# A depthwise convolution's products moved from GpSimd to ScalarE, and attention's values transposed one projection tile earlier

## The chip, the cores and the metric

One core of one Trainium2 chip runs the whole program in one launch. The metric is the time of an execution on the device in microseconds (us); of several runs the median is given. The profile is that of one execution.

## What is computed

Two transformer blocks in fp32 on 256 tokens of width 1024. The first block (two kinds of attention, cross-attention to a memory, 16 experts) is not touched. The second has two layers, and each layer's mixer projects its normed input to 2560 columns, from which four parallel mixers are fed. Layer 0 works on 512 tokens (256 of the sequence and 256 of the context), layer 1 on the 256 of the sequence. The change concerns the convolution mixer and, beside it, the projection that feeds all four:

```python
def conformer_conv(u, w_dw, b_dw, ln_g, ln_b):
    a, gate = jnp.split(u, 2, axis=-1)
    h = a * jax.nn.sigmoid(gate)
    h = lax.conv_general_dilated(h, w_dw, window_strides=(1,),
                                 padding=((CONV_K // 2, CONV_K // 2),),
                                 dimension_numbers=('NWC', 'WIO', 'NWC'),
                                 feature_group_count=CONV_CH) + b_dw
    return jax.nn.silu(layernorm(h, ln_g, ln_b))
```

It is depthwise: 256 channels, 31 taps. With the channels in two halves of 128 partitions, each half is a sum of 31 shifted copies of its input, each times one weight per partition.

## The kernel before

Every engine has an instruction list of its own, written out by hand in Python (`@block.tensor`, `@block.scalar`, `@block.vector`, `@block.gpsimd`, and SyncE, which only issues loads); the lists are in order and meet through semaphores. A `Signal` is a semaphore with named counts: `mark` adds to it when an instruction ends, `at` is what a wait needs.

**Projections.** Weights come in tiles of 1024 x 256 fp32, 1 MB each. SyncE loads them in a fixed order into five slots of `raw`, each as soon as the tile five places before is used (`load_tiles`, L617). ScalarE copies a tile to a rounded high part `w_hi` (`act_feed`, L654), VectorE subtracts it for the low part `w_lo` (`dve_feed`, L666), both up to two tiles ahead of TensorE, and TensorE multiplies in three products per chunk (`products`, L677 to L679). The results of a tile stand in one of two pairs of PSUM banks and ScalarE evicts them (`act_tile`, L1640); TensorE may start a tile when the one two places before is evicted. Each layer of the second block has ten such tiles `("win2", l, j)` in the order `W2_ORDER` = 2, 3, 0, 1, 4, 5, 6, 7, 8, 9. Tiles 2 and 3 are the two halves of the convolution's input: after them ScalarE takes the sigmoid (`act_glu`, L2053) and VectorE multiplies (`dve_glu`, L2061) into `conv_in` (`sq` in the profile).

**Convolution.** From place 3 of that order on, VectorE has the taps of the first half of the channels, four or five for every tile, as one multiply-and-add each (`dve_taps`, L1410). GpSimd has those of the second half (`pool_taps`): one multiply with the bias for tap 0 (L1432), then 30 times a multiply into the buffer `term` (L1434) and an add to the sum (L1435), each waiting for the one before. GpSimd does nothing else then. All taps are 512 columns wide in layer 0 and 256 in layer 1; sums and term buffer are parts of `proj`. The layer norm that follows them stands at step 22 of layer 0's attention and step 6 of layer 1's (`plan_layernorm`).

**Values.** Tile 1 holds keys and values of one of the mixers. After the tenth tile TensorE transposes the values (`pe_values_turned`, L2041, four transposes into bank 5), ScalarE copies them out (`act_values`, L2046), and TensorE waits for that copy, for the last tile's eviction, the last rotary embedding and GpSimd's bias (L2420 to L2424) before attention begins.

**Attention.** A unit is a pair of score matrices. At step i (`pe_attention`, `act_attention`, `dve_attention`) TensorE computes the scores of unit i (L1164), transposes the probabilities of unit i-2 (L1181) and multiplies those of unit i-3 with the values (L1198). VectorE takes the maximum of unit i out of PSUM (L1239) and scales the probabilities of unit i-1, for the differential heads with L1260 (one head's map, times minus lambda) and L1262 (the other's, plus the first). ScalarE does the exponentials of unit i (L1211) and copies unit i-2's transposes out (L1223). Between them, at the steps 0 to 7 of layer 0, TensorE multiplies a 1 MB tile of the modulation's weights per step (`pe_ada`, L785), straight from its slot of `raw`; after the eighth the sums go over ScalarE (L811) and back to TensorE (L800). Layer 0 has such tiles again at steps 17 to 20, layer 1 at steps 0 to 3. The first units of layer 0 are those of the context's 256 tokens: eight differential pairs, then eight others.

## Time and profile before

| | us |
|---|---|
| median of three runs | 1669.44 (1666.41 to 1669.54) |
| the profiled execution | 1663.33 |
| its span | 1661.6 |
| TensorE busy | 1593.2 (96%), weight loads 1360.8 (82%) |
| VectorE, ScalarE, GpSimd busy | 891.7, 675.0, 214.9 |
| GpSimd's taps, both layers | 162.5 of these (L1432, L1434, L1435) |
| mean granted clock | 0.988 |

Times in the rows are counted from the start of the span. Engines are PE (TensorE), PEld (its weight loads), DVE (VectorE), ACT (ScalarE), POOL (GpSimd), SP (SyncE). A row such as "L1260 DVE TENSOR_SCALAR work<-work,small 128x256 ... x8 | 9.9, 1242 | 0.3" reads: line, engine, operation, out<-in, shape, count; busy us in total, mean ns of one; the engine's idle time just before them, and after an arrow what ended it. A timeline row has start, duration (from the first start to the last end where it stands for several), and in brackets the idle time before it.

### The profile page before, as it was taken

The page shows a single profiled execution, that of the slowest core. Times are in us where ns is not written, and L with a number is a line of the kernel's source. Part 1 is how long each engine was busy: PE and PEld are TensorE (multiplying, and loading weights), DVE is VectorE, ACT ScalarE, POOL GpSimd, SP SyncE. Part 2 cuts the span into 40 slices and gives each one's busy share as a digit, 9 for nine tenths or more (in the row PEclk, how much of TensorE's full clock was granted, in tenths as well). Part 3 has the DMA queues.
Part 4 walks back from the last instruction along what each step waited for, and adds up shares of the span by engine and source line. Part 5 has one row for each costly group of instructions (what it writes and reads, how often), then busy time and mean ns, then how long its engine had stood idle before and what let it go on. Part 6 is the DMA issues. An engine that isn't in the chain of part 4 may idle for free.

```text
span 1661.6 us, 24572 instructions
## 1 busy us (share of the span) xinstructions
PE 1593.2 (96%) x10537; PEld 1360.8 (82%) x10537; DVE 891.7 (54%) x1198; ACT 675.0 (41%) x974; POOL 214.9 (13%) x206
## 2 busy tenths in 40 slices
PE   7999999999999999978999999999998998899998
PEld 6976997998888888944677888888877975799998
DVE  4623663756544566977725333333327668465554
ACT  5536533444544434146633322221225226543433
POOL 3001000000000016980200000000001860000000
PEclk9999999999999999999999999999999999999999
DMA  9577557566565634373142433233244351355552
GB/s 290 153 250 232 171 176 237 154 188 197 162 206 180 197 88 151 102 228 102 11 117 77 127 102 96 86 98 101 89 139 128 102 170 34 102 178 179 184 181 67
DMA packets 228916, 242.18 MB, mean 146 GB/s; under 512 B 13064, under 2 KB 222440, under 8 KB 228808
## 3 DMA queue, kind: packets, MB, share of 16 engines
q1 hardware_dynamic: 226672, 238.03, 44.7%
q0 software_dynamic: 1600, 2.37, 2.4%
q8 instruction: 83, 1.36, 0.4%
q10 hardware_dynamic: 536, 0.22, 0.1%
q14 instruction: 25, 0.20, 0.0%
HBM read 239.55 MB, written 1.05 MB: 145 GB/s over the span
## 4 chain that ended last, share of the span: by engine, by line
PE 85%; DVE 8%; ACT 4%; issue 1%; DMA 1%; SPq 1%; DVEq 0%; ACTq 0%
PE bank L677 18%; PE bank L679 18%; PE bank L678 18%; PE bank L1817 4%; PE bank L1824 4%; PE bank L1823 3%; PE score_banks L1164 2%; PE score_banks L1890 2%; PE score_banks L1891 2%; PE score_banks L1892 2%; DVE small L1239 2%; PE bank L1198 2%; PE bank L750 1%; PE bank L752 1%; PE bank L751 1%
## 5 line engine op out<-in xcount | busy, mean ns | idle before, releaser
L666 DVE TENSOR_TENSOR w_lo<-raw,w_hi 128x2048 fp32r<-128x2048 f32 (+1 forms) x147 | 338.8, 2307 | 232.6 <-ACT w_hi L654 232.1
L677 PE MATMUL bank<-xn_hi,w_hi 128*128 128x256 f32 (+1 forms) x1232 | 407.3, 331 | 5.5 <-ACT proj L1640 3.1
L678 PE MATMUL bank<-xn_lo,w_hi 128*128 128x256 f32 (+1 forms) x1232 | 404.3, 328 | 0.0
L679 PE MATMUL bank<-xn_hi,w_lo 128*128 128x256 f32 (+1 forms) x1232 | 404.3, 328 | 0.0
L654 ACT ACTIVATE w_hi<-raw 128x2048 fp32r<-128x2048 f32 (+1 forms) x147 | 277.2, 1887 | 156.1 <-PE bank L679 97.8
L677 PEld LDWEIGHTS bank<-xn_hi,w_hi 128*128 128x128 f32 x1232 | 235.7, 191 | 27.5 <-issue 5.0
L678 PEld LDWEIGHTS bank<-xn_lo,w_hi 128*128 128x128 f32 x1232 | 235.9, 191 | 19.9
L679 PEld LDWEIGHTS bank<-xn_hi,w_lo 128*128 128x128 f32 x1232 | 235.7, 191 | 20.0
L677 PE MATMUL bank<-hid_hi,w_hi 128*128 128x256 f32 (+1 forms) x416 | 137.5, 330 | 2.6 <-DVE hid_lo L1722 1.9
L678 PE MATMUL bank<-hid_lo,w_hi 128*128 128x256 f32 (+1 forms) x416 | 136.4, 328 | 0.0
L679 PE MATMUL bank<-hid_hi,w_lo 128*128 128x256 f32 (+1 forms) x416 | 136.4, 328 | 0.0
L1211 ACT ACTIVATE work<-score_banks,small 128x512 f32<-128x512 f32 (+2 forms) x120 | 68.7, 577 | 104.6 <-DVE small L1239 84.2
L1657 DVE SCALAR_TENSOR_TENSOR xT<-bank,mod,xT 128x256 f32<-128x256 f32 x96 | 40.6, 478 | 129.0 <-PE bank L679 116.7
L1640 ACT ACTIVATE proj<-bank 128x512 f32<-128x512 f32 (+1 forms) x60 | 31.4, 558 | 179.2 <-PE bank L679 163.1
L1817 PE MATMUL bank<-w_hi,hid_hi 128*128 128x512 f32 x256 | 102.0, 398 | 0.0
L1239 DVE TENSOR_REDUCE small<-score_banks 128x2 f32<-128x1024 f32 (+3 forms) x64 | 57.9, 905 | 79.9 <-PE score_banks L1164 41.5
L1824 PE MATMUL bank<-w_hi,hid_lo 128*128 128x512 f32 x256 | 100.2, 391 | 0.0
L1793 DVE TENSOR_TENSOR w_lo<-raw,w_hi 128x2048 fp32r<-128x2048 f32 (+1 forms) x36 | 67.0, 1876 | 42.9 <-ACT w_hi L1786 42.8
L677 PEld LDWEIGHTS bank<-hid_hi,w_hi 128*128 128x128 f32 x416 | 79.1, 190 | 11.8 <-DVE hid_lo L1722 3.0
L1434 POOL TENSOR_SCALAR proj<-sq,vec 128x512 f32<-128x512 f32 (+1 forms) x60 | 87.0, 1450 | 5.9
L679 PEld LDWEIGHTS bank<-hid_hi,w_lo 128*128 128x128 f32 x416 | 79.1, 190 | 7.0
L678 PEld LDWEIGHTS bank<-hid_lo,w_hi 128*128 128x128 f32 x416 | 79.1, 190 | 6.7
(336 smaller groups left out, 2724.6 us busy)
## 6 DMA issues: line engine op xcount, KB each, us to landing
raw<-in_w_ada SPq DMA_DIRECT2D x48, 1024.0 KB, 5.7
raw<-in_w_in SPq DMA_DIRECT2D x30, 1024.0 KB, 6.3
raw<-in_w_gate SPq DMA_DIRECT2D x22, 1024.0 KB, 5.4
raw<-in_w_up SPq DMA_DIRECT2D x22, 1024.0 KB, 5.5
raw<-in_w_exp_up SPq DMA_DIRECT2D x16, 1024.0 KB, 7.6
raw<-in_w_exp_gate SPq DMA_DIRECT2D x16, 1024.0 KB, 9.6
raw<-in_w_exp_down SPq DMA_DIRECT2D x16, 1024.0 KB, 5.0
raw<-in_w_down SPq DMA_DIRECT2D x16, 1024.0 KB, 5.2
```

The costliest lines, as they stand in the source:

```text
L654: act.activation(w_hi[:, i % HIGH_SLOTS, 0:k * cols], raw[:, r % RAW_SLOTS, 0:k * cols], ACT.Copy)\
L666: dve.tensor_tensor(w_lo[:, r % RAW_SLOTS, 0:k * cols], raw[:, r % RAW_SLOTS, 0:k * cols], w_hi[:, i % HIGH_SLOTS, 0:k * cols].bitcast(F32 ...
L677: pe.matmul(o, s_hi, m_hi, start=i == 0, stop=False)
L678: pe.matmul(o, s_hi, m_lo, start=False, stop=False)
L679: last = pe.matmul(o, s_lo, m_hi, start=False, stop=i == n - 1)
L1211: last = act.activation(prob(s)[:, 0:nk], score_bank(unit, s)[:, 0:nk], ACT.Exp, bias=nmax(s), accum_out=rsum(s))
L1239: ins = dve.tensor_reduce(nmax(s0, n), src, AX.X, ALU.max, negate=True)
L1434: own.ready(pool.tensor_scalar(term, src(1, k), w, None, ALU.mult))
L1793: last = dve.tensor_tensor(lo, w, hi.bitcast(F32), ALU.subtract)
L1817: pe.matmul(halves_of, x_hi[:, c, ts], hi, start=c == 0, stop=False, skip_group_check=True)
L1823: pe.matmul(halves_of, x_hi[:, c, ts], lo, start=False, stop=False, skip_group_check=True)
L1824: last = pe.matmul(halves_of, x_lo[:, c, ts], hi, start=False, stop=c == KC - 1, skip_group_check=True)
```

## The change

On ScalarE, `act_terms` multiplies the 30 taps 1 to 30 of the second half, in thirteen bunches: before and after the eviction of each of the tiles from place 3 on, but the last, which has only the bunch before. The terms alternate between two buffers in `conv_d` (a part of `proj`); term k waits for the add of term k-2. GpSimd keeps tap 0 and adds each term when it is ready. On TensorE and ScalarE the values are turned and copied after the tile at place 8, the ninth, and TensorE waits for the last tile's eviction at step 1 of attention, behind the scores of the second unit and ahead of that step's modulation products. VectorE's list is the same.

```diff
+VALUES_AT = 8
...
+        def term(l, k):
+            return conv_d[:, k % 2, 0:2 if l == 0 else 1, :]
+
+        def act_terms(act, l, bunch):
+
+            _, _, src = conv_views(l)
+            n = 2 * (len(W2_ORDER) - CONV_FROM) - 1
+            first, last = (1 + (CONV_K - 1) * min(bunch + i, n) // n for i in range(2))
+            if first == 1:
+                act.wait_ge(*dve_misc.at(("glu", l)))
+            for k in range(first, last):
+                w = vec[:, 1, l * 62 + 2 * k + 1:l * 62 + 2 * k + 2]
+                if k >= 3:
+                    act.wait_ge(*term_added.at((l, k - 2)))
+                act.activation(term(l, k), src(1, k), ACT.Copy, scale=w).then_inc(*term_ready.mark((l, k)))
+
         def pool_taps(pool, l):
 
             own = Step(pool, pool_step)
-            ns, acc, src = conv_views(l)
-            term = conv_d[:, 1, 0:ns, :]
-            for k in range(CONV_K):
-                w = vec[:, 1, l * 62 + 2 * k + 1:l * 62 + 2 * k + 2]
-                if k == 0:
-                    b = VEC_AT["conv_b_2"] + 2 * l + 1
-                    own.ready(pool.tensor_scalar(acc(1), src(1, 0), w, vec[:, 0, b:b + 1], ALU.mult, ALU.add))
-                else:
-                    own.ready(pool.tensor_scalar(term, src(1, k), w, None, ALU.mult))
-                    ins = pool.tensor_tensor(acc(1), acc(1), term, ALU.add)
-                    if k < CONV_K - 1:
-                        own.ready(ins)
-            ins.then_inc(*pool_done.mark(("conv", l)))
+            _, acc, src = conv_views(l)
+            w, b = vec[:, 1, l * 62 + 1:l * 62 + 2], VEC_AT["conv_b_2"] + 2 * l + 1
+            own.ready(pool.tensor_scalar(acc(1), src(1, 0), w, vec[:, 0, b:b + 1], ALU.mult, ALU.add))
+            for k in range(1, CONV_K):
+                pool.wait_ge(*term_ready.at((l, k)))
+                pool.tensor_tensor(acc(1), acc(1), term(l, k), ALU.add).then_inc(*term_added.mark((l, k)))
+                pool.wait_ge(*term_added.at((l, k)))
...
-                pe.wait_ge(*pool_done.at(("conv", l)))
+                pe.wait_ge(*term_added.at((l, CONV_K - 1)))
...
-                pe_values_turned(pe, l)
-                pe.wait_ge(*act_out.at(("win2", l, 9)))
+                    if place == VALUES_AT:
+                        pe_values_turned(pe, l)
                 pe.wait_ge(*dve_misc.at(("rope", l, 6)))
                 pe.wait_ge(*act_misc.at(("values", l)))
                 pe.wait_ge(*pool_done.at(("bias", l)))
 
                 def fill(i, l=l):
                     run_plan(l, "pe")(pe, i)
+                    if i == 1:
+                        pe.wait_ge(*act_out.at(("win2", l, W2_ORDER[-1])))
...
-                for j in W2_ORDER:
-                    act_tiles(act, [("win2", l, j)])
+                for place, j in enumerate(W2_ORDER):
+                    act_feed(act, ("win2", l, j))
+                    if place >= CONV_FROM:
+                        act_terms(act, l, 2 * (place - CONV_FROM))
+                    act_tile(act, ("win2", l, j))
                     if j == 3:
                         act_glu(act, l)
-                act_values(act, l)
+                    if place == VALUES_AT:
+                        act_values(act, l)
+                    if place >= CONV_FROM:
+                        act_terms(act, l, 2 * (place - CONV_FROM) + 1)
```

How this moves instructions, at three places. (Lines of the kernel after it are numbered anew: L1640 is L1653 there, L654 is L657, L2046 is L2059, L1435 is L1450, L2041 is L2054, L1164 is L1167, L785 is L788, and L677 to L679 are L680 to L682.)

ScalarE, the last projection tiles of layer 0, before: high parts of weights (L654), evictions (L1640, two pieces a tile, so that x6 is three tiles), values (L2046), then attention's exponentials.

```order
L654 ACTIVATE w_hi<-raw 128x2048
L1640 ACTIVATE proj<-bank 128x512 x2
L654 ACTIVATE w_hi<-raw 128x2048
L1640 ACTIVATE proj<-bank 128x512 x2
L654 ACTIVATE w_hi<-raw 128x2048
L1640 ACTIVATE proj<-bank 128x512 x6
L2046 ACTIVATE work<-score_banks 128x512
L1211 ACTIVATE work,small<-score_banks,small 128x256 x6
```

After, with the terms of the convolution (L1440):

```order
L1653 ACTIVATE proj<-bank 128x512 x2
L1440 ACTIVATE proj<-sq,vec 128x512 x2
L657 ACTIVATE w_hi<-raw 128x2048
L1440 ACTIVATE proj<-sq,vec 128x512 x2
L1653 ACTIVATE proj<-bank 128x512 x2
L1440 ACTIVATE proj<-sq,vec 128x512 x5
L1653 ACTIVATE proj<-bank 128x512 x2
L2059 ACTIVATE work<-score_banks 128x512
L1440 ACTIVATE proj<-sq,vec 128x512 x5
L1653 ACTIVATE proj<-bank 128x512 x2
L1214 ACTIVATE work,small<-score_banks,small 128x256 x6
```

The terms stand in bunches of two to five around the evictions of L1653, and the values ahead of the last of these.

GpSimd, the start of layer 0's taps, with what each waits for, before:

```order
L2328 TENSOR_TENSOR aux<-aux,cst 128x2048 [waits bias_loaded]
L1432 TENSOR_SCALAR proj<-sq,vec 128x512 [waits dve_misc]
L1434 TENSOR_SCALAR proj<-sq,vec 128x512 [waits pool_step]
L1435 TENSOR_TENSOR proj<-proj 128x512 [waits pool_step]
L1434 TENSOR_SCALAR proj<-sq,vec 128x512 [waits pool_step]
L1435 TENSOR_TENSOR proj<-proj 128x512 [waits pool_step]
L1434 TENSOR_SCALAR proj<-sq,vec 128x512 [waits pool_step]
```

After:

```order
L2338 MEMSET sq 128x1144 [waits moment_ready,xn_ready]
L2341 TENSOR_TENSOR aux<-aux,cst 128x2048 [waits bias_loaded]
L1447 TENSOR_SCALAR proj<-sq,vec 128x512 [waits dve_misc]
L1450 TENSOR_TENSOR proj<-proj 128x512 [waits term_ready,pool_step]
L1450 TENSOR_TENSOR proj<-proj 128x512 [waits term_ready,term_added] x29
L2333 DMA aux<-in_na_rpb 64x4x64 [waits scores_ready,term_added]
```

Multiply and add took turns before, each after the one before it; now thirty adds stand in a row, each waiting for its term (`term_ready`) and for the add before it (`term_added`).

TensorE, from the tenth tile of layer 0 into attention, before:

```order
L677 MATMUL bank<-w_hi,xn_hi 128x256
L678 MATMUL bank<-w_lo,xn_hi 128x256
L679 MATMUL bank<-w_hi,xn_lo 128x256
L2041 MATMUL score_banks<-cst,proj 128x128 x4
L1164 MATMUL score_banks<-proj 128x256 x2
L785 MATMUL bank<-raw,cond 32x256 x8
L1164 MATMUL score_banks<-proj 128x256 x2
L785 MATMUL bank<-raw,cond 32x256 x8
```

After, around the end of the ninth tile:

```order
L680 MATMUL bank<-xn_hi,w_hi 128x512
L681 MATMUL bank<-xn_lo,w_hi 128x512
L682 MATMUL bank<-xn_hi,w_lo 128x512
L2054 MATMUL score_banks<-cst,proj 128x128 x4
L680 MATMUL bank<-w_hi,xn_hi 128x256
L681 MATMUL bank<-w_lo,xn_hi 128x256
L682 MATMUL bank<-w_hi,xn_lo 128x256
```

And at the end of the tenth:

```order
L682 MATMUL bank<-w_hi,xn_lo 128x256
L680 MATMUL bank<-w_hi,xn_hi 128x256
L681 MATMUL bank<-w_lo,xn_hi 128x256
L682 MATMUL bank<-w_hi,xn_lo 128x256
L1167 MATMUL score_banks<-proj 128x256 x2
L788 MATMUL bank<-raw,cond 32x256 x8
L1167 MATMUL score_banks<-proj 128x256 x2
```

The four transposes of the values stood between the tenth tile and the first scores, and stand between the ninth tile and the tenth.

## Rows read from the trace of the kernel before

**Rows 1.** The page: shares of the chain that ended last, by engine.

```profile
PE 85%; DVE 8%; ACT 4%; issue 1%; DMA 1%; SPq 1%; DVEq 0%; ACTq 0%
```

**Rows 2.** Windows, core 0: length, busy (count) per engine, PEclk, DMA share, GB/s.

```profile
640.00:702.00 62.00, 62.00 (x328) 53.69 (x327) 55.50 (x52) 13.74 (x16) 58.91 (x35) 1.00 0.27 87
...
714.00:735.00 21.00, 16.51 (x188) 7.50 (x184) 19.19 (x28) 9.31 (x36) 19.73 (x15) 1.00 1.04 329
...
738.00:741.00 3.00, 1.00 (x8) 0.70 (x5) 2.89 (x6) 1.66 (x7) 2.82 (x3) 0.84 1.06 338
741.00:747.00 6.00, 6.00 (x28) 3.43 (x28) 4.16 (x15) 3.54 (x14) 0.55 (x1) 0.51 0.14 45
```

**Rows 3.** Waits of TensorE, 708 to 745 us: total, times, longest.

```profile
PE bank L1181 <- DVE work L1262: 5.4, 7, 0.9
PE bank L800 <- ACT ada_sums L811: 2.0, 1, 2.0
```

**Rows 4.** Chain of work, 700 to 760 us: start, us, engine, tile, line.

```profile
722.21 1.41 DVE work L1260
723.64 0.88 DVE work L1262
...
725.23 1.41 DVE work L1260
```

**Rows 5.** VectorE's groups by form, 711 to 741.5, then 741.5 to 783 us.

```profile
L1239 DVE TENSOR_REDUCE small<-score_banks 128x2 f32<-128x512 f32 x10 | 6.8, 681 | 8.5 <-PE score_banks L1164 8.5
...
L1262 DVE SCALAR_TENSOR_TENSOR work<-work,small 128x512 f32<-128x512 f32 x6 | 4.5, 751 | 0.2
L1239 DVE TENSOR_REDUCE small<-score_banks 128x2 f32<-128x512 f32 x6 | 4.1, 688 | 3.6 <-PE score_banks L1164 3.5
L1260 DVE TENSOR_SCALAR work<-work,small 128x512 f32<-128x512 f32 x6 | 3.3, 546 | 0.2
```

**Rows 6.** GpSimd's groups by form, whole span, then its timeline from 736 us.

```profile
L1434 POOL TENSOR_SCALAR proj<-sq,vec 128x512 f32<-128x512 f32 x30 | 52.6, 1754 | 3.0
L1435 POOL TENSOR_TENSOR proj<-proj 128x512 f32<-128x512 f32 x30 | 44.8, 1492 | 2.5
...
740.29 1.26 POOL L1435 TENSOR_TENSOR proj<-proj 128x512 f32<-128x512 f32 x1
```

**Rows 7.** ScalarE's groups, 640 to 711 us, then two evictions of its timeline.

```profile
L654 ACT ACTIVATE w_hi<-raw 128x2048 fp32r<-128x2048 f32 x4 | 7.7, 1916 | 0.0
L1640 ACT ACTIVATE proj<-bank 128x512 f32<-128x512 f32 x12 | 6.5, 596 | 52.7 <-PE bank L679 52.7
...
700.31 1.09 ACT L1640 ACTIVATE proj<-bank 128x512 f32<-128x512 f32 x2 [9.79 <-PE bank L679]
711.82 1.08 ACT L1640 ACTIVATE proj<-bank 128x512 f32<-128x512 f32 x2 [10.43 <-PE bank L679]
```

**Rows 8.** Timelines of layer 1: GpSimd's last add, TensorE's first scores.

```profile
1356.57 0.73 POOL L1435 TENSOR_TENSOR proj<-proj 128x256 f32<-128x256 f32 x1
...
1359.01 1.13 PE L1164 MATMUL score_banks<-proj 32*128 32x512 f32 x4 [1.43 <-ACT work L2046]
```

**Rows 9.** TensorE's timeline, layer 0: where units' scores start.

```profile
713.65 0.70 PE L1164 MATMUL score_banks<-proj 32*128 32x256 f32 x4 [1.43 <-ACT work L2046]
...
735.00 0.70 PE L1164 MATMUL score_banks<-proj 64*128 64x256 f32 x4
...
747.71 0.70 PE L1164 MATMUL score_banks<-proj 64*128 64x256 f32 x4
...
751.23 0.70 PE L1164 MATMUL score_banks<-proj 64*128 64x256 f32 x4
...
753.03 0.70 PE L1164 MATMUL score_banks<-proj 64*128 64x256 f32 x4
```

**Rows 10.** Loads issued by SyncE from 718 to 721 us, and time to landing.

```profile
L629 SPq DMA_DIRECT2D raw<-in_w_ada x1: 729/729/729, 720.0 to 720.0; - x1
...
DMA to landing us min/median/max: 9.5/9.5/9.5
```

More of the change, by code:

```diff
@@ L349, in mixer_program @@
         hidden_turned = signal("hidden_turned")
+        term_ready = signal("term_ready")
+        term_added = signal("term_added")
         shown = signal("shown")
```

## The prediction

> **What bounds the kernel now.** First the page: 85% of the chain that ended last is TensorE [rows 1], so an edit on ScalarE or GpSimd pays only where TensorE stands still. Then the windows around the convolution of layer 0 [rows 2]. While the projections run (640 to 702 us, and on to 711) TensorE is busy without a gap: whatever the change does to other engines there is worth nothing, unless it starves TensorE. From 714 to 741 TensorE has gaps, VectorE is full (19.19 of 21 us, 2.89 of the last 3), GpSimd is still at its taps, and the DMA share is 1.04 and more. From 741 to 747 the granted clock is 0.51, the lower level (1.2 GHz); TensorE had been busy for 1.00 of the 3 us before.
>
> The table of waits names what TensorE waits for there: VectorE's L1262, 5.4 us in seven waits, and the modulation's sums, 2.0 us [rows 3]. The chain of work agrees: in that stretch it is L1239, L1260, L1262, L1239 and so on, all VectorE, 3.02 us from one L1260 to the next [rows 4].
>
> Why is VectorE slow there? L1260 takes 1.41 us on 256 columns and L1262 0.87 [rows 4]. On 512 columns, with GpSimd silent, they take 0.546 and 0.751; L1239, the reduction out of PSUM, takes 0.681 with GpSimd at work and 0.688 without [rows 5]. GpSimd's last add runs from 740.29 to 741.55 [rows 6]. So GpSimd's taps hold up VectorE's work in SBUF for 27 us of layer 0's attention.
>
> **GpSimd (removed: 30 multiplies a layer).** Layer 0 has 30 multiplies of 1.754 us and 30 adds of 1.492 [rows 6]: 97.4 us. The adds alone are 44.8 us, and ScalarE's bunches pace them: two or three terms before and after each tile's eviction, 4.6 a tile. The last five stand between the values and the last tile's eviction. They can start after the eviction of 700.31 and the values, at some 702.3; five adds of 1.5 us with 0.1 between end at about 710.3, before the last tile does at 711.8 [rows 7]. In layer 1 GpSimd ended at 1357.3 and the first scores began at 1359.01 [rows 8]: nothing to win there.
>
> **ScalarE (added: 30 terms a layer).** A 512-wide copy takes it 0.596 us [rows 7], so layer 0 adds 17.9 us, and layer 1, with half the columns, no more. Cover: 52.7 us of waiting for tiles in layer 0 [rows 7], and waits of the same kind in layer 1. Without it evictions and the feeding of weights, which stand in the same queue, come late. The pace to keep: 11.5 us between evictions [rows 7] less 1.09 and 1.92 for the tile's own copy and high part leaves 8.5 us for 4.6 terms, 1.8 each. An add of 1.5 us fits, since there are two term buffers. I take zero. VectorE's taps get quicker, beside a TensorE that is busy anyway: zero.
>
> **Values turned earlier.** The four transposes stay on TensorE, one tile sooner; what goes is the wait behind them, 1.43 us in each layer [rows 8, 9]. The last tile's eviction is now awaited only after the second unit's scores. Without the 1.43 us the first scores start at 712.2 and are over at 712.9; the eviction is over at 711.82 + 1.09 = 712.9 [rows 7], two groups before anyone asks. Behind that wait stand only step 1's products for the modulation. **-1.4 us in each layer.**
>
> **Units 0 to 7 of layer 0.** A free VectorE step is at most 0.71 (from L1262's end to the next L1260, [rows 4]) + 0.55 (L1260) + 0.75 (L1262), 2.0 us, since these two are prices of 512 columns, against 3.02. TensorE's own work from the first scores (713.65) to the ninth unit's (735.00) is 21.35 us [rows 9] less 4.5 of waiting (21.00 - 16.51, [rows 2]): 16.85, 2.1 a step. So TensorE sets the step, and the 4.5 us go. Late next is the DMA. Eight tiles of modulation weights are used, four lie ready; the others come at about 345 GB/s [rows 2], 3.04 us each. The eighth, issued at 720.0, landed 9.5 us later, at 729.5 [rows 10]. TensorE would want it at 712.2 + 16.85 - 1.0 = 728.1. Earlier use issues it sooner, but more transfers then share the engines: 714 + 4 x 3.04 = 726.2 at best, 730.5 at worst. I take 1.3 us of waiting. **-4.5 + 1.3 = -3.2 us.**
>
> The Trainium skill (SBUF — State Buffer, section "SBUF: two separate sides") gives DMA a peak of about 436 GB/s. By that a tile takes 2.4 us, the eighth is in by 724, the 1.3 us are not lost, and the sum is -9.5 instead of -8.2. The trace has a full share at 338 to 348 GB/s, so the row decides.
>
> **Units 8 to 11 (735.00 to 747.71).** These 12.7 us hold waits of 0.9 and 2.0 us [rows 3] and 6.0 busy us at a clock of 0.51 [rows 2], which are 3.0 us of work at the full one. Bounds: all of it goes, -5.9; or only the wait on L1262, -0.9. Nearest are the next steps, of the same kind with GpSimd silent at full clock: 3.5 us (a norm's eight products among them) and 1.8 [rows 9]; I take 2.2 a step. Four of these, 0.7 for turning the sums (four products, like L1164's) and 1.0 of waiting for them, half of today's (they come behind two exponentials), make 10.5. **-2.2 us.**
>
> **Sum:** -1.4 - 3.2 - 2.2 - 1.4 = **-8.2 us**. The profiled execution took 1663.33 us (span 1661.6, 1.7 around it): 1655.1. It lay 6.1 us under the median of the runs shown, 1669.44; against that the answer is **1661.2 us**.
>
> **Rivals.**
> - *The transfers set the step (0.20).* The eighth tile lands at 730.5, unit 8 starts at 731.7 instead of 735.0 (-3.3, the values included), and the clock still falls (-0.9). With layer 1's 1.4: -5.6, 1663.8. For it: a DMA share over 1.0 throughout. Against: four tiles lie ready.
> - *TensorE stays ahead and keeps its clock (0.15).* 1.4 + 4.5 + 5.9 + 1.4 = -13.2, 1656.2. For it: the clock fell behind the longest gaps, which shrink. Against: the transfers, as above.
> - *Only the values count (0.10).* Either GpSimd is not what holds up VectorE, or its adds are not over when attention begins. -2.9, 1666.5. Against it: L1239 is the same in both stretches, and the change of pace falls on GpSimd's end. The Trainium skill (SBUF — State Buffer, section "Who interferes with whom") has VectorE and GpSimd share a port pair that scaling in SBUF and two-input work can be blocked on, and a reduction never; the trace agrees, 1.41 us against 0.681, which is why this has only 0.10.
> - *The hand-over between ScalarE and GpSimd starves TensorE: slower (0.05).* If term and add do not overlap, a term costs 1.5 + 0.6 + two signals of 0.1 = 2.3 us, over the 1.8 that decides. Each of six tiles then takes ScalarE 3.0 + 4.6 x 2.3 = 13.6 us instead of 11.5, the last eviction is 12.6 us late and TensorE waits for it at step 1; against that stand the 3.2 and 2.2 us that attention still wins, so about +7 us, 1676.5. For it: one in-order queue holds terms, feeds and evictions. Against: a term needs only the add two before.
>
> **How the numbers follow.** The forecast has 0.50, with -6 to -10.5 us as its own range. A measurement of this kernel can tell about 0.2%, 3.3 us, from no change. Faster: 0.50 + 0.20 + 0.15 = 0.85; same 0.10; slower 0.05. The range goes from 1655.5, just past the best case, to 1667.0, which takes in the transfers' case and the values alone. Left out are the slower case and the tails that the spread of the runs (3.1 us over three) puts beyond either end.
>
> **What would show it.** Right: GpSimd's last add of layer 0 ends before TensorE's last projection tile; L1260 on 256 columns takes 0.3 to 0.4 us; no wait for turned values; TensorE's waits on L1262 under 1 us in sum before unit 8, with 1 to 2 us for the weights' DMA in their place; no gap of TensorE in either layer's projections. Wrong: GpSimd busy past the first scores; L1260 near 1.4 us with GpSimd silent; TensorE waiting for a w_lo in the projections; or a lowered clock later on that gives the time back.

## The result and the profile after

| | before | after |
|---|---|---|
| median, runs of the same comparison | 1667.93 us (1665.93 to 1669.54, 4 runs) | 1653.99 us (1651.27 to 1656.91, 4 runs) |
| the profiled execution, its span | 1663.33, 1661.6 | 1651.99, 1650.3 |
| TensorE busy | 1593.2 | 1592.3 |
| VectorE, ScalarE, GpSimd busy | 891.7, 675.0, 214.9 | 885.5, 707.1, 128.8 |
| mean granted clock | 0.988 | 0.988 |

The ratio is 0.9916 (0.989 to 0.9941): faster by 13.9 us. The forecast was 8.2 us faster, 1661.2 with a range of 1655.5 to 1667.0. The sign is right, and the result lies 1.5 us below the range. Two further comparisons of the same kernel, below, gave 0.994 and 0.9923, with medians of 1655.15 and 1653.39 us.

In the profile after, the changed lines have new numbers: L1164 is now L1167, L1181 is L1184, L1239 is L1242, L1260 is L1263, L1262 is L1265, L1640 is L1653, L654 is L657, L800 and L811 are L803 and L814, L1435 is L1450, and L1440 is ScalarE's term.

The page's chain that ended last, shares by engine, after [rows 1]:

```profile
PE 86%; DVE 6%; ACT 4%; issue 1%; DMA 1%; SPq 1%; DVEq 0%; ACTq 0%
```

Windows of the kernel after, in the columns of [rows 2]:

```profile
640.00:702.00 62.00, 62.00 (x341) 54.14 (x340) 59.55 (x53) 29.93 (x42) 38.84 (x25) 1.00 0.31 102
702.00:709.00 7.00, 7.00 (x61) 6.87 (x59) 4.46 (x4) 1.46 (x2) 5.30 (x4) 1.00 0.01 2
709.00:726.00 17.00, 16.80 (x193) 8.04 (x192) 12.07 (x29) 10.48 (x39) 0.00 (x0) 1.00 0.98 318
726.00:736.00 10.00, 8.09 (x56) 4.71 (x52) 7.32 (x28) 6.11 (x27) 0.00 (x0) 0.83 1.09 347
```

TensorE has no gap in the projections, as before. From the first scores on, TensorE is busy for 16.80 of 17 us where it had 16.51 of 21, and the granted clock stays at 1.00; VectorE is no longer full (12.07 of 17 against 19.19 of 21), and GpSimd does nothing. The DMA share is close to full in both (0.98, then 1.09).

TensorE's timeline after, where the units' scores start (first, ninth, eleventh and thirteenth unit of layer 0), and the one product between them that waits; columns: start, us, engine, line:

```profile
708.94 0.70 PE L1167 MATMUL score_banks<-proj 32*128 32x256 f32 x4
...
725.66 0.70 PE L1167 MATMUL score_banks<-proj 64*128 64x256 f32 x4
...
729.24 0.62 PE L803 MATMUL bank<-cst,ada_sums 128*128 128x16 f32 x4 [1.29 <-ACT ada_sums L814]
...
730.05 0.70 PE L1167 MATMUL score_banks<-proj 64*128 64x256 f32 x4
...
736.01 0.70 PE L1167 MATMUL score_banks<-proj 64*128 64x256 f32 x4
```

Before, the same three starts stood at 713.65, 735.00 and 747.71 [rows 9]: 21.35 and 12.71 us. Now they are 16.72 and 10.35 us. That is **-4.63 for units 0 to 7 and -2.36 for units 8 to 11**. The wait of 1.43 us before the first scores is gone in this layer and in the other, **-1.43 twice**.

Waits of TensorE after, 705 to 745 us [rows 3]:

```profile
PE bank L1184 <- ACT prob_turned L1226: 1.4, 3, 0.6
PE bank L803 <- ACT ada_sums L814: 1.3, 1, 1.3
PE bank L1184 <- DVE work L1265: 0.2, 1, 0.2
```

The 5.4 us on VectorE's second scaling are 0.2. What is left is the wait for the sums, 1.29 us, and three short ones on ScalarE, 1.4 together. No load is waited for: the eighth tile of modulation weights, one row of the loads that SyncE issues from 714 to 716 us [rows 10] and its time to landing:

```profile
L632 SPq DMA_DIRECT2D raw<-in_w_ada x1: 739/739/739, 714.6 to 714.6; - x1
...
DMA to landing us min/median/max: 9.5/9.5/9.5
```

714.6 + 9.5 = 724.1, and TensorE's first product with it starts at 724.66. The clock and other pieces of the span, in windows after, then before:

```profile
276.00:289.00 13.00, 11.10 (x90) 10.73 (x91) 5.71 (x7) 5.78 (x8) 0.00 (x0) 1.00 0.35 101
...
1243.00:1281.00 38.00, 35.25 (x224) 30.83 (x223) 29.31 (x48) 22.88 (x36) 6.45 (x4) 0.82 0.40 130
```

```profile
276.00:289.00 13.00, 10.33 (x64) 9.80 (x64) 4.12 (x5) 5.34 (x6) 0.00 (x0) 0.74 0.37 116
...
1243.00:1281.00 38.00, 33.98 (x222) 29.21 (x221) 26.03 (x51) 19.22 (x30) 2.23 (x2) 0.98 0.52 152
```

Here one profile against another misleads. Before had a lowered clock at 276 to 289 us (0.74), 350 us ahead of anything that was changed; the profile after does not, and is 2.3 us ahead for it. At 1243 to 1281 us it is the other way round (0.82 against 0.98). Paired product by product, TensorE is 11.4 us ahead of before at 1243 us and 9.2 at 1300: 2.2 us go back, in the two other profiles of the change as well. The difference of the two profiled executions, 11.34 us, therefore holds more than the change. The four pieces that the prediction priced have -1.43 - 4.63 - 2.36 - 1.43 = **-9.85 us**, where it had -8.2. They are not the whole: from layer 0's first scores to the end of the span it is 948.0 us before and 941.4 after, which with the first 1.43 makes -8.0 us, and -7.5 in each of the other two profiles. What the four pieces win beyond that is lost later, above all from 1243 us on.

VectorE's groups by form, 709 to 736 us, after [rows 5]:

```profile
L1242 DVE TENSOR_REDUCE small<-score_banks 128x2 f32<-128x512 f32 x12 | 8.3, 690 | 9.0 <-PE score_banks L1167 9.0
L1265 DVE SCALAR_TENSOR_TENSOR work<-work,small 128x256 f32<-128x256 f32 x8 | 3.9, 484 | 0.3
L1263 DVE TENSOR_SCALAR work<-work,small 128x256 f32<-128x256 f32 x8 | 3.3, 412 | 0.3
```

With GpSimd silent the two scalings of 256 columns take 0.41 and 0.48 us, against 1.41 and 0.88 in the steps of [rows 4]; the reduction out of PSUM stays at 0.69 (0.68 before, [rows 5]).

GpSimd's groups by form over the whole span, after, and its last rows of the timeline in layer 0 [rows 6]:

```profile
L1450 POOL TENSOR_TENSOR proj<-proj 128x512 f32<-128x512 f32 x30 | 46.7, 1557 | 25.3 <-ACT proj L1440 23.7
L1450 POOL TENSOR_TENSOR proj<-proj 128x256 f32<-128x256 f32 x30 | 26.2, 872 | 36.0 <-ACT proj L1440 34.5
```

```profile
699.44 8.10 POOL L1450 TENSOR_TENSOR proj<-proj 128x512 f32<-128x512 f32 x5 [2.77 <-ACT proj L1440]
```

The last add ends at 707.5, 1.4 us before the first scores.

ScalarE's groups by form, 640 to 709 us, after [rows 7]:

```profile
L1440 ACT ACTIVATE proj<-sq,vec 128x512 f32<-128x512 f32 x28 | 19.3, 724 | 8.9 <-POOL proj L1450 8.9
...
L1653 ACT ACTIVATE proj<-bank 128x512 f32<-128x512 f32 x11 | 6.0, 596 | 24.6 <-PE bank L682 24.6
```

A term takes 0.724 us, not 0.596. 28 of them are 19.3 us, another 8.9 us are waits for GpSimd's adds, and of the 52.7 us of waiting for tiles 24.6 are left: enough.

VectorE's taps beside them did not get quicker: from 640 to 702 us a multiply-and-add of the first half takes 1.244 us on average (28 of them), against 1.211 before (26). The pace of term and add, where ScalarE waits for GpSimd, in its timeline after:

```profile
700.77 0.73 ACT L1440 ACTIVATE proj<-sq,vec 128x512 f32<-128x512 f32 x1 [0.86 <-POOL proj L1450]
702.47 0.73 ACT L1440 ACTIVATE proj<-sq,vec 128x512 f32<-128x512 f32 x1 [0.97 <-POOL proj L1450]
```

One tap takes 1.70 us, from 700.77 to 702.47.

### The profile page after: what moved, and what is told of

It is laid out like the page before. It is cut to its first block, busy times and chain, and to the rows that moved or that the text cites. A ratio compares the mean times of both kernels' runs of the same rounds, so it can differ in the third digit from the quotient of the medians.

```text
span 1650.3 us, 24634 instructions
## 1 busy us (share of the span) xinstructions
PE 1592.3 (96%) x10537; PEld 1359.5 (82%) x10537; DVE 885.5 (54%) x1198; ACT 707.1 (43%) x1034; POOL 128.8 (8%) x146
## 4 chain that ended last, share of the span: by engine, by line
PE 86%; DVE 6%; ACT 4%; issue 1%; DMA 1%; SPq 1%; DVEq 0%; ACTq 0%
PE bank L680 18%; PE bank L682 18%; PE bank L681 18%; PE bank L1830 4%; PE bank L1837 4%; PE bank L1836 3%; PE score_banks L1167 2%; PE score_banks L1903 2%; PE score_banks L1904 2%; PE score_banks L1905 2%; PE bank L1201 2%; DVE small L1242 1%; DVE w_lo L669 1%; PE bank L788 1%; PE bank L753 1%
## 5 line engine op out<-in xcount | busy, mean ns | idle before, releaser
L680 PE MATMUL bank<-xn_hi,w_hi 128*128 128x256 f32 (+1 forms) x1232 | 406.9, 330 | 5.3 <-ACT proj L1653 3.1
L682 PE MATMUL bank<-xn_hi,w_lo 128*128 128x256 f32 (+1 forms) x1232 | 404.0, 328 | 0.0
L657 ACT ACTIVATE w_hi<-raw 128x2048 fp32r<-128x2048 f32 (+1 forms) x147 | 277.1, 1886 | 155.7 <-PE bank L682 97.8
L680 PEld LDWEIGHTS bank<-xn_hi,w_hi 128*128 128x128 f32 x1232 | 235.4, 191 | 27.1 <-issue 4.6
L682 PEld LDWEIGHTS bank<-xn_hi,w_lo 128*128 128x128 f32 x1232 | 235.4, 191 | 20.2
L680 PE MATMUL bank<-hid_hi,w_hi 128*128 128x256 f32 (+1 forms) x416 | 137.5, 331 | 2.6 <-DVE hid_lo L1735 1.9
L682 PE MATMUL bank<-hid_hi,w_lo 128*128 128x256 f32 (+1 forms) x416 | 136.4, 328 | 0.0
L1242 DVE TENSOR_REDUCE small<-score_banks 128x2 f32<-128x1024 f32 (+3 forms) x64 | 58.0, 906 | 77.0 <-PE score_banks L1167 38.8
L680 PEld LDWEIGHTS bank<-hid_hi,w_hi 128*128 128x128 f32 x416 | 79.0, 190 | 11.8 <-DVE hid_lo L1735 3.0
L1653 ACT ACTIVATE proj<-bank 128x512 f32<-128x512 f32 (+1 forms) x60 | 31.4, 558 | 132.4 <-PE bank L682 116.9
L682 PEld LDWEIGHTS bank<-hid_hi,w_lo 128*128 128x128 f32 x416 | 79.1, 190 | 7.0
L1836 PE MATMUL bank<-w_lo,hid_hi 128*128 128x512 f32 x208 | 81.1, 390 | 0.0
```

Source lines behind the costliest of these rows:

```text
L657: act.activation(w_hi[:, i % HIGH_SLOTS, 0:k * cols], raw[:, r % RAW_SLOTS, 0:k * cols], ACT.Copy)\
L680: pe.matmul(o, s_hi, m_hi, start=i == 0, stop=False)
L682: last = pe.matmul(o, s_lo, m_hi, start=False, stop=i == n - 1)
L1242: ins = dve.tensor_reduce(nmax(s0, n), src, AX.X, ALU.max, negate=True)
L1836: pe.matmul(halves_of, x_hi[:, c, ts], lo, start=False, stop=False, skip_group_check=True)
```

## The experiments

Two theories of where the gain is from. The **hold**: GpSimd's work in SBUF holds up VectorE's, and what pays is only that GpSimd is done when attention begins; the values' wait adds its 1.43 us a layer. **Elsewhere**: the gain comes from elsewhere (from the values alone, or by where the clock falls), and the rest is chance. Further questions: do ScalarE's terms cost anything, is it GpSimd's multiplies or its adds that hold VectorE, and what do the sums' wait and the clock behind it still cost? Each expectation names for itself the theories that it sets against each other.

### The change once more

The kernel after, unchanged.

> The whole change again, timed against the kernel before in five rounds. Theory (GpSimd's multiplies held up VectorE in layer 0's attention, and TensorE with it; the values' wait is gone in both layers): the stage's own part is 1.4 + 4.6 + 2.4 + 0.6 in layer 0 and 1.4 in layer 1, so -10 to -11 us, ratio 0.9935. Rival (the four runs show the true size, some further gain lies outside these stages): -14 us, ratio 0.9916.

Measured: 1655.15 us (1652.37 to 1658.71) against 1665.6 (1660.76 to 1671.21, 25 runs), ratio 0.994 (0.9919 to 0.996). The stage's lengths, from the first scores to the ninth unit's and to the thirteenth's, are 16.71 and 11.10 us. And once more on another chip:

> The change itself once more, to stand beside turn_later_again on the same chip. Theory 1 (the stage gives about 9.5 us, the rest of the first result was where the clock happened to fall): a ratio of 0.994, 0.992 to 0.996. Theory 2 (the first result, 0.9916, was the change's own worth): 0.992 or under. In the profile: from the first scores of layer 0 to the ninth unit's 16.7 us, from there to the thirteenth's 10.3 to 11.1.

Measured: 1653.39 us (1652.11 to 1654.62) against 1665.77 (11 runs), ratio 0.9923 (0.9901 to 0.9944); 16.71 and 11.09 us. What follows: the stage repeats to 0.01 us in its first part and within 0.8 us in its second, while single executions of one kernel differ by up to 7 us (the change) and 13 us (before). The three ratios are 0.9916, 0.994 and 0.9923; 0.9937, the product of the two halves below, lies in the interval of each. So does 0.9923, and the third comparison does not decide between a worth of 0.994 and one of 0.9916.

### The values alone

```diff
+VALUES_AT = 8
...
+                    if place == VALUES_AT:
+                        pe_values_turned(pe, l)
-                pe_values_turned(pe, l)
-                pe.wait_ge(*act_out.at(("win2", l, 9)))
...
+                    if place == VALUES_AT:
+                        act_values(act, l)
```

The edit is made on the kernel before; the convolution is as it was there. As in the change, the last tile's eviction is awaited at step 1 of attention (not shown in the cut above).

> Only the values are turned a tile earlier; GpSimd's taps as before. Theory: the wait of 1.43 us goes in each layer, but in layer 0 VectorE, still held up, sets the end of unit 8, so the 1.4 us are kept only if its whole row of steps starts earlier: -2.9 us, ratio 0.998. Rival (VectorE's pace takes it back, or the change's gain is mostly this): 0 to -1.5 us, or below -5.

Measured: 1661.98 us (12 runs) against 1665.6, ratio 0.9979 (0.9965 to 0.9994): -3.5 us (-1.0 to -5.8), 2.9 by the waits that go. The stage stays long, 19.97 and 12.69 us. The first part is 1.4 us shorter than before, but this is lost again behind the twelfth unit: from the first scores of layer 0 to the last it is 106.8 us, against 106.7 before. Waits of TensorE, 708 to 745 us, of this kernel:

```profile
PE bank L1182 <- DVE work L1263: 4.1, 7, 0.9
PE bank L801 <- ACT ada_sums L812: 2.0, 1, 2.0
```

L1263 is here the second scaling, L1262 of before: with GpSimd at its taps TensorE still waits for VectorE. The measured gain fits the wait that went, and the theory that it is the whole gain of the change falls. That the values are worth just this is not shown: the one profile of this kernel, from layer 0's first scores to the end of the span, is 1.5 us longer than that of before, as much as the first wait had won.

### The terms alone

```diff
-                    if place == VALUES_AT:
-                        pe_values_turned(pe, l)
+                pe_values_turned(pe, l)
+                pe.wait_ge(*act_out.at(("win2", l, 9)))
...
-                    if place == VALUES_AT:
-                        act_values(act, l)
+                act_values(act, l)
```

This one is made on the kernel after, and undoes the move of the values, the wait at step 1 with it.

> Only ScalarE's terms and GpSimd's adds; values turned after the last tile as before. Theory: -4.6 - 2.4 - 0.6 = -7.6 us, up to -9, ratio 0.995; L1263's like on 256 columns near 0.41 us, GpSimd silent before the first scores. Rival (parts are not additive, the terms win only with the values moved): under -4 us.

Measured: 1658.91 us (8 runs) against 1665.6, ratio 0.9958 (0.994 to 0.9976): -7.0 us (-4.0 to -10.0). Stage: 16.72 and 10.35 us, exactly those of the profile after, whose difference to before is 4.63 + 2.36 = 7.0. The values' wait is back:

```profile
PE score_banks L1167 <- ACT work L2059: 1.4, 1, 1.4
```

The halves multiply to 0.9979 x 0.9958 = 0.9937: **-10.5 us**. The four pieces in the trace gave -9.85, the whole of the trace behind the first changed instruction -7.5 to -8.0; the intervals of the halves do not tell these apart.

### Do ScalarE's terms cost anything?

```diff
-                    own.ready(pool.tensor_scalar(term, src(1, k), w, None, ALU.mult))
+                    if k == 1:
+                        own.ready(pool.tensor_scalar(term, src(1, k), w, None, ALU.mult))
```

On the kernel before: behind tap 0 GpSimd multiplies only once and adds 30 times, so the convolution's second half is not computed. ScalarE has nothing added.

> The kernel before with GpSimd's multiplies of taps 2 to 30 left out (the sum adds tap 1's product again and again, so the convolution's second half isn't computed); ScalarE does nothing more than before. Theory: GpSimd ends near 683 us, attention is as with the terms on ScalarE, -7.6 us, within 1 us of the kernel with the terms alone, which says what ScalarE's 30 terms a layer cost. Rival (ScalarE's terms cost something behind TensorE's cover): this one is faster than the terms alone by over 2 us. Rival (GpSimd isn't what holds VectorE): no change.

Measured: 1659.77 us (12 runs), ratio 0.9966 (0.9949 to 0.9983), as terms_only within the intervals. VectorE's scalings from 711 to 736 us are those of the kernel after:

```profile
L1262 DVE SCALAR_TENSOR_TENSOR work<-work,small 128x256 f32<-128x256 f32 x8 | 3.9, 485 | 0.3
L1260 DVE TENSOR_SCALAR work<-work,small 128x256 f32<-128x256 f32 x8 | 3.3, 413 | 0.3
```

GpSimd's last add ends at 688.6 us. So less work on GpSimd gives the gain of terms_only by itself, and ScalarE's terms cost nothing that shows: the two medians differ by 0.9 us, with the terms on the faster side. A cost of one or two us would be hidden in the intervals. The profiled execution had a lowered clock at the start of the stage, with TensorE busy throughout, so the length of its stage (22.61 and 9.13 us) says nothing on that; its window there:

```profile
712.00:726.00 14.00, 14.00 (x94) 5.64 (x94) 6.64 (x16) 5.60 (x23) 0.00 (x0) 0.51 0.96 309
```

### GpSimd kept busy into the attention

On the kernel after, GpSimd goes on after its add 29 of layer 0, in the term buffer that is free by then; nothing of the result changes. Three forms: ten pairs of a multiply and an add, 22 adds, 18 multiplies.

```diff
+                if (l, k) == (0, CONV_K - 2):
+                    spare = term(l, k)
+                    for i in range(10):
+                        own.ready(pool.tensor_scalar(spare, src(1, i), w, None, ALU.mult))
+                        own.ready(pool.tensor_tensor(spare, spare, acc(1), ALU.add))
```

> The whole change, but in layer 0 GpSimd does ten more pairs of a multiply and an add into the spare term buffer, between its last two adds, so that it works on into attention as before (nothing of the result depends on them). Theory (GpSimd's work in SBUF holds up VectorE's): L1263 on 256 columns goes from 0.41 back to 1.2 to 1.4 us, a step to 3.0, and 5 to 7 us of the change are lost: ratio near 0.998. Rival (the gain of the stage comes from the order of the work or the clock, not from GpSimd's silence): L1263 stays near 0.4 and the ratio at 0.994.

Measured: 1660.73 us (12 runs) against 1666.26 (17 runs), ratio 0.9971 (0.9955 to 0.9988). The stage is back at its length before: 20.94 and 13.66 us against 21.35 and 12.71. VectorE's groups from 711 to 736 us, GpSimd's from 700 to 745 us (L1455 and L1456 are the pairs) and TensorE's waits from 708 to 745 us, of this kernel:

```profile
L1263 DVE TENSOR_SCALAR work<-work,small 128x256 f32<-128x256 f32 x7 | 8.8, 1258 | 0.3
L1242 DVE TENSOR_REDUCE small<-score_banks 128x2 f32<-128x512 f32 x9 | 6.1, 681 | 4.1 <-PE score_banks L1167 4.1
L1265 DVE SCALAR_TENSOR_TENSOR work<-work,small 128x256 f32<-128x256 f32 x7 | 6.0, 863 | 0.2
```

```profile
L1455 POOL TENSOR_SCALAR proj<-sq,vec 128x512 f32<-128x512 f32 x10 | 16.0, 1605 | 1.0
L1456 POOL TENSOR_TENSOR proj<-proj 128x512 f32<-128x512 f32 x10 | 12.7, 1272 | 0.8
```

```profile
PE bank L1184 <- DVE work L1265: 5.0, 7, 0.9
PE bank L803 <- ACT ada_sums L814: 2.0, 1, 2.0
```

This is the clearest run: everything of the change is in it, VectorE and TensorE have the same instructions, and only GpSimd is at work for 29 us more. Of the change's 10 to 14 us 4.8 remain by the ratio (2.0 to 7.5), 5.5 by the medians; 2.9 of them are the values', and the rest is within the interval. The hold is shown, with the reduction out of PSUM (0.68 us) again untouched.

The other two were executed once each:

> The same with 22 adds in place of the ten pairs, one look. Theory A (any GpSimd instruction that reads SBUF holds VectorE): L1263 1.2 us or more, L1265 0.8 or more. Theory B (the multiplies alone do it, adds let VectorE through): L1263 near 0.4, L1265 near 0.5, and TensorE's units 0 to 8 in 16.7 us.

> The same with 18 multiplies in place of the ten pairs, one look. Theory A: L1263 1.2 us or more, as with the adds. Theory B: L1263 1.4 us or more here and not with the adds.

Measured: 1664.83 us with the adds and 1660.92 with the multiplies. VectorE's groups from 711 to 736 us, of the kernel with adds, then of that with multiplies:

```profile
L1265 DVE SCALAR_TENSOR_TENSOR work<-work,small 128x256 f32<-128x256 f32 x6 | 8.6, 1439 | 0.2
L1242 DVE TENSOR_REDUCE small<-score_banks 128x2 f32<-128x512 f32 x8 | 5.5, 687 | 8.4 <-PE score_banks L1167 8.4
L1263 DVE TENSOR_SCALAR work<-work,small 128x256 f32<-128x256 f32 x6 | 4.9, 824 | 0.2
```

```profile
L1242 DVE TENSOR_REDUCE small<-score_banks 128x2 f32<-128x512 f32 x11 | 7.6, 687 | 5.7 <-PE score_banks L1167 5.4
L1265 DVE SCALAR_TENSOR_TENSOR work<-work,small 128x256 f32<-128x256 f32 x8 | 5.3, 659 | 0.3
L1263 DVE TENSOR_SCALAR work<-work,small 128x256 f32<-128x256 f32 x8 | 4.8, 605 | 0.3
```

Neither kind alone repeats the pattern of the taps. Beside adds VectorE's operation with two inputs takes 1.44 us on average instead of 0.48, that with one input 0.82 instead of 0.41. Beside multiplies they take 0.66 and 0.61, and TensorE hardly feels them: the first eight units take 17.61 us, 0.9 more than with GpSimd silent.

These averages depend on where in GpSimd's instruction VectorE's begins, as single instructions show. GpSimd's and VectorE's rows of the timeline beside each other, first with the pairs:

```profile
717.47 1.27 POOL L1456 TENSOR_TENSOR proj<-proj 128x512 f32<-128x512 f32 x1
717.50 1.40 DVE L1263 TENSOR_SCALAR work<-work,small 128x256 f32<-128x256 f32 x1
718.85 1.56 POOL L1455 TENSOR_SCALAR proj<-sq,vec 128x512 f32<-128x512 f32 x1
718.93 0.88 DVE L1265 SCALAR_TENSOR_TENSOR work<-work,small 128x256 f32<-128x256 f32 x1
```

Then with adds alone, and with multiplies alone:

```profile
728.20 1.27 POOL L1455 TENSOR_TENSOR proj<-proj 128x512 f32<-128x512 f32 x1
728.10 1.52 DVE L1263 TENSOR_SCALAR work<-work,small 128x256 f32<-128x256 f32 x1
```

```profile
717.40 1.56 POOL L1455 TENSOR_SCALAR proj<-sq,vec 128x512 f32<-128x512 f32 x1
718.02 0.41 DVE L1263 TENSOR_SCALAR work<-work,small 128x256 f32<-128x256 f32 x1
```

In the pairs L1263 begins 0.03 us after an add, ends 0.16 us after it, and so takes 1.40 us; L1265 then falls into the multiply and takes 0.88. A step of VectorE and a pair of GpSimd both last 3.02 us, so it is the same in six steps running, and in the kernel before too (L1260 from 722.21, GpSimd's add from 722.19). With adds alone one L1263 that met the start of an add took 1.52 us; five others met one in its course, took 0.57 to 0.97 and ended, like the first, 0.15 or 0.16 us after it; with multiplies alone L1263 took 0.41 to 0.82, and the one shown ran inside a multiply at its free 0.41. So it is the add that holds the one-input operation to the add's end. What the taps' alternation did was to bring VectorE to the start of an add at every step.

That 1664.83 is so high is in part the clock, which in this one execution was at 0.53 from 717 to 735 us: its stage (26.25 us) is no price of the adds.

```profile
717.00:735.00 18.00, 17.47 (x119) 7.25 (x112) 13.81 (x18) 6.15 (x25) 16.94 (x14) 0.53 0.98 313
```

### The sums turned one step later

TensorE turns the first batch of modulation sums at step 10 instead of 9, and VectorE takes them up a step later too.

```diff
-                    ada_turn_left.append((b, step))
+                    ada_turn_left.append((b, step + (ADA_BATCHES[b]["names"][0] == ADA_PLAN[("mix", 0), 0][0])))
...
-                dve_ada(dve, ada_planned(("mix", l), i - 2))
+                late = l == 0 and i in (9, 10)
+                dve_ada(dve, [] if late and i == 9 else ada_planned(("mix", l), i - 3 if late else i - 2))
```

> The whole change, and the modulation's sums of layer 0's first eight tiles are turned at step 10 of attention instead of step 9 (VectorE takes them a step later too). Theory (TensorE's 1.29 us wait for the sums is the next loss of this stage, and its being idle there is what lets the clock fall): -1.3 us against the whole change, up to -3 where the clock stays up, ratio 0.992 to 0.993. Rival (another wait takes its place, or the clock falls anyway): 0.994, the same as the whole change.

Measured: 1651.41 us (6 runs), ratio 0.9928 (0.9901 to 0.9956). Once more, beside the third comparison of the change:

> The change with the first batch of modulation sums turned one step later. Theory 1 (the wait of 1.3 us for the sums, and the fall of the clock behind it, are the last 2 us that this stage has): 1.5 to 2.5 us under whole_third, a ratio of 0.9925 to 0.993 against before. Theory 2 (one step later only moves the wait): as whole_third within 1 us. In the profile: units 8 to 11 of layer 0 take 8.7 us, against 10.3 or more.

Measured: 1651.92 us (1649.68 to 1654.12, 5 runs), ratio 0.9915 (0.9893 to 0.9938), against 1653.39 for the change itself on the same chip. Windows of this kernel, and then of the change in the run beside it:

```profile
727.00:736.00 9.00, 7.55 (x66) 4.21 (x56) 7.83 (x29) 6.72 (x28) 0.00 (x0) 1.00 1.09 349
```

```profile
727.00:737.00 10.00, 8.71 (x48) 5.12 (x48) 6.81 (x25) 5.38 (x23) 0.00 (x0) 0.66 1.09 348
```

The sums are not waited for any more, the clock of the stretch is 1.00 instead of 0.66, and the eight units take 16.72 and the next four 8.69 us (8.70 in the first run). The change has 11.09, 11.10 and 10.35 us there in its three profiles, so 1.7 to 2.4 us are won. The profiled executions differ by 2.25 us, the medians by 1.5 us, and the runs overlap: the gain shows in the traces, while the ratios (0.9928 and 0.9915) can't be told from the change's.

## Why the prediction was right or wrong

- **What bounds the stage: right.** VectorE's operations in SBUF were held up by GpSimd's taps. Shown from both sides: with less work on GpSimd they fall to 0.41 and 0.48 us (the prediction had 0.3 to 0.4 for the first), with the work put back they rise to 1.26 and 0.86 us. The sentences of the Trainium skill (SBUF — State Buffer, section "Who interferes with whom") bore this out in kind: the reduction never moved. Its section speaks of a lock for the whole of an instruction, with the other engine fully blocked. GpSimd's adds behave so (L1263 ended 0.16 us after the add that it met at its start); its multiplies do not, since L1263 ran inside one in its free 0.41 us, and there the measurement decides.
- **The values, -1.4 in each layer: right in the trace of the change.** The wait is gone in both. By themselves the two measured -3.5 (-1.0 to -5.8) for 2.9. The last eviction awaited at step 1 was never waited for.
- **ScalarE's terms, zero: right, with a wrong size.** 0.724 us each where a copy out of PSUM takes 0.596 [rows 7]. A copy with a scale per partition out of SBUF is another operation; I had taken the nearest row. It cost nothing, since the cover was large.
- **VectorE's taps would get quicker: wrong, and it costs nothing.** 1.244 against 1.211 us a tap. That adds hold an operation with two inputs more than multiplies do is what the two busy kernels show; that this is why the taps stayed slow was not tried.
- **GpSimd's end: right.** 707.5 against 710.3, in a trace that was 3.2 us ahead by then, before anything that was changed.
- **Units 0 to 7: the step that failed is "I take 1.3 us of waiting".** The 4.5 us went (4.63 measured); the wait for the weights that was to take their place is in none of the profiles. I had set the eighth tile's landing at a fixed time of the span, 726.2 to 730.5, and its use at 728.1. But loads are issued when slots come free, so they move with the stage. Counted from the first scores, the load was issued 6.35 us in and landed at 15.85 before [rows 9, 10]; after, it is issued 5.7 us in and lands at 15.2. TensorE's use stands 15.9 us in by the prediction's own figures, 15.7 measured. The rows said that it would be in time, by nothing; it was in time by 0.5 us. The Trainium skill's peak for DMA (SBUF — State Buffer, section "SBUF: two separate sides"), set against the row of 338 to 348 GB/s, gave the better sum of the two here but for the wrong reason: the transfers moved 309 to 349 GB/s in the windows shown. (Of the prediction's rates, [rows 2] shows 329 and 338 GB/s; 348 is the window from 735 to 738 us.)
- **Units 8 to 11, -2.2: right**, -2.36 in the profile, -1.6 in two others, according to whether the clock falls for a shorter or a longer time behind the sums' wait, which went from 2.0 to 1.29 us ("1.0 of waiting").
- **The range: too short at its low end, and its middle stood too high.** The sum was set against 1669.44, the median of three runs. The 57 runs of the kernel before that stand beside all comparisons have a median of 1666.0 and reach from 1658.6 to 1671.2. So three runs had said 3.4 us too much, and the profiled execution (1663.33), from which the shift of 6.1 us was taken, was nearer. The low end held only the best case of the stage itself, at 1656.2, and 0.7 us below it for a spread of single runs that is 5 to 7 us to either side. With the term of the wait left out (-9.5) and the better anchor the forecast would have been 1656.5. So of the 7.2 us between 1661.2 and the measured 1653.99 the wait explains 1.3, the other terms of the stage 0.3, and the anchor 3.4; the last 2.2 no run explains. All three medians of the change (1653.99, 1655.15, 1653.39) lie under the low end, so it was not one lucky comparison.
- **A lowered clock later on that gives time back** was named as what could undo the gain. In all three profiles of the change the stretch from 1243 to 1281 us has a clock of 0.82 instead of 0.98, and 2.2 us are given back by 1300 us. Before has 0.98, values_only and terms_only 0.96; busy_pairs has 0.89 and gives back the same 2.2. So neither half of the change has it alone, and GpSimd's silence is not its cause; what is stays open. The sum of the four pieces leaves it out.
- **Of the rivals** the hand-over never starved TensorE: an add and its term run at 1.70 us a tap when ScalarE waits for GpSimd, below the 1.8 that decided. The case that TensorE stays ahead and keeps its clock was half true: ahead it stayed, its clock it kept throughout only in turn_later, where the whole comes to 1.43 + 4.63 + 4.01 + 1.43 = 11.5 us, 1.7 short of this rival's 13.2.

What stays open: the three comparisons of the change lie at -14.0, -10.0 and -12.8 us (their ratios times 1666), the halves at -10.5, the four pieces in the trace at -9.85, and the whole trace behind the first changed instruction at -7.5 to -8.0. The intervals of the three reach from -6.7 to -18.3. The one profile of the kernel before was 2.7 us quicker than the median of its 57 runs, and where those lose the 2.7 us no trace shows; with them the trace would come to some -10.5. The 8.0 us come near the forecast's 8.2, in part by luck: the stage won 1.65 us more than the forecast, and the 2.2 us that went back behind it were in no term.

## What to carry to other kernels

When one engine's slow stretch ends with another engine's work, ask first which operation is being held, by comparing an operation that reads PSUM with one that reads SBUF in both stretches; then take work away from the engine that holds, even if it is itself never waited for. Times of loads belong on the clock of the stage that frees their slots, not on that of the span. And put the forecast's anchor and range on the spread of many runs: here single executions of one kernel differ by up to 13 us, as much as the whole change.

## What the runs showed of the hardware that was not expected

- How long GpSimd holds VectorE depends on GpSimd's operation and on where in it VectorE's begins, not on GpSimd's being busy. VectorE's operation with one input (256 columns, SBUF to SBUF) took 0.41 us alone and 0.41 to 0.82 beside multiplies; beside adds it ended 0.15 or 0.16 us after the add that it met, and took up to 1.52. That with two inputs took 0.48 alone, 0.48 to 0.87 beside multiplies and about 1.44 beside adds. In alternation the two engines fell into the same 3.02 us, and VectorE paid 1.40 and 0.88 at every step.
- GpSimd's multiply by a weight per partition takes longer than its add of two tensors: 1.60 against 1.27 us (512 columns, in the pairs of busy_pairs), though it has one input less.
- ScalarE's copy with a scale per partition of 512 columns in SBUF takes 0.72 us, the one out of PSUM 0.60; it ran beside VectorE and GpSimd at work, and TensorE had no gap. Its time with those two silent was not measured.
- In the 10 us with TensorE's wait of 1.3 us for the sums, beside smaller ones, the granted clock was 0.66 to 0.83; with that wait gone it stayed at 1.00, and 1.7 to 2.4 us came back for a wait of 1.3.
